# Expert rows gathered in quarters and turned by VectorE in blocks of 32x32

## What is computed

```python
for e in range(N_EXPERTS):
    he = jax.nn.silu(xt @ w_gate[e]) * (xt @ w_up[e])
    y = y + combine[:, e:e + 1] * (he @ w_down[e])
```

## Time and profile before

| what | value |
|---|---|
| median of the runs | 1838.65 us (three runs, 1836.47 to 1839.16) |
| span of the profiled execution | 1837.4 us |
| expert stage, first to last step | about 1526 to 1807 us |
| TensorE busy over the span | 1760.4 us (96%) |
| VectorE busy | 858.7 us (47%) |
| GpSimd busy | 235.1 us (13%) |

### The profile page before, as it was taken

The page is one execution under the profiler, slowest core; times in us unless marked ns, Lnnn a source line. Parts: engine busy times, 40 slices in busy tenths (PEclk is TensorE's granted clock), DMA queues, the critical chain, the costliest instruction groups (busy, mean ns, idle before and its releaser), DMA issues. The chain is left out here.

```text
span 1837.4 us, 22565 instructions
## 1 busy us (share of the span) xinstructions
PE 1760.4 (96%) x9024; PEld 1289.9 (70%) x9024; DVE 858.7 (47%) x1672; ACT 627.8 (34%) x1248; POOL 235.1 (13%) x286
## 2 busy tenths in 40 slices
PE   7999999999999999999999999999999989999993
PEld 6778888888888787568888888888766663333330
DVE  4436544543367345745554453263347562333224
ACT  5236344323353224635433332253347320000001
POOL 4000000000001003310000000000014404333322
PEclk9999999999999998999999999999999999999997
DMA  7223333332232217303333322332320158999974
GB/s 236 90 76 84 100 91 91 97 109 92 92 121 92 69 65 228 111 25 91 92 95 109 93 92 92 104 127 91 93 92 24 55 228 330 376 398 389 380 311 151
DMA packets 179528, 261.02 MB, mean 142 GB/s; under 512 B 18904, under 2 KB 134824, under 8 KB 167152
## 3 DMA queue, kind: packets, MB, share of 16 engines
q1 hardware_dynamic: 155824, 204.66, 33.2%
q0 software_dynamic: 19584, 25.77, 4.4%
q10 hardware_dynamic: 4032, 29.36, 4.1%
HBM read 297.53 MB, written 29.40 MB: 178 GB/s over the span
## 5 line engine op out<-in xcount | busy, mean ns | idle before, releaser
L189 PE MATMUL PB<-RING_R,OPS_R 128*128 128x512 f32 (+1 forms) x1056 | 414.7, 393 | 5.1 <-DVE RING_R L152 4.1
L191 PE MATMUL PB<-RING_R,OPS_R 128*128 128x512 f32 (+1 forms) x1056 | 409.1, 387 | 0.0
L190 PE MATMUL PB<-RING_R,OPS_R 128*128 128x512 f32 (+1 forms) x1056 | 408.9, 387 | 0.0
L169 DVE SCALAR_TENSOR_TENSOR RING_R<-RING,gains,RING_R 128x256 fp32r<-128x256 f32 (+2 forms) x456 | 219.4, 551 | 253.8 <-ACT RING_R L167 253.8
L189 PE MATMUL PB<-OPS_R,RING_R 128*128 128x512 f32 (+1 forms) x736 | 280.7, 381 | 0.0
L190 PE MATMUL PB<-OPS_R,RING_R 128*128 128x512 f32 (+1 forms) x736 | 279.5, 380 | 0.0
L191 PE MATMUL PB<-OPS_R,RING_R 128*128 128x512 f32 (+1 forms) x736 | 279.5, 380 | 0.0
L189 PEld LDWEIGHTS PB<-RING_R,OPS_R 128*128 128x128 f32 x1056 | 198.8, 188 | 48.4 <-DVE RING_R L152 5.3
L167 ACT ACTIVATE RING_R<-RING,gains 128x256 fp32r<-128x256 f32 (+2 forms) x456 | 209.9, 541 | 59.2 <-DMA RING<-in_w_in 47.7
L191 PEld LDWEIGHTS PB<-RING_R,OPS_R 128*128 128x128 f32 x1056 | 198.8, 188 | 40.7
L190 PEld LDWEIGHTS PB<-RING_R,OPS_R 128*128 128x128 f32 x1056 | 199.0, 188 | 38.9 <-issue 0.2
(11 more groups left out here) (379 smaller groups left out, 2033.1 us busy)
## 6 DMA issues: line engine op xcount, KB each, us to landing
RING<-in_ffn_w_gate SPq DMA_DIRECT2D x44, 512.0 KB, 4.0
RING<-in_ffn_w_up SPq DMA_DIRECT2D x44, 512.0 KB, 5.2
RING<-in_ffn_w_down SPq DMA_DIRECT2D x44, 512.0 KB, 4.2
RING<-in_w_expert_gate SPq DMA_DIRECT2D x16, 1024.0 KB, 8.0
RING<-in_w_expert_up SPq DMA_DIRECT2D x16, 1024.0 KB, 11.6
OPS<-in_w_expert_gate SPq DMA_DIRECT2D x16, 1024.0 KB, 13.6
OPS<-in_w_expert_up SPq DMA_DIRECT2D x16, 1024.0 KB, 16.2
Y<-in_w_expert_down ACTq DMA_DIRECT2D x14, 1024.0 KB, 9.6
```

The lines of the kernel that those rows point to most:

```text
L169: t = nc.vector.scalar_tensor_tensor(by_k(RING_R, o)[:, :, k, :], raw, g, high.bitcast(fp32), ALU.mult, ALU.subtract)
L189: nc.tensor.matmul(o, x[0], w[0], start=start, stop=False)
L190: nc.tensor.matmul(o, x[0], w[1], start=False, stop=False)
L191: return nc.tensor.matmul(o, x[1], w[0], start=False, stop=stop)
```

## The change

The rows are stored in their natural order (no stepped read any more). From step 2 on a pair's rows are not gathered as 128 rows of 4 KB but as four times 128 quarters of 1 KB: in DMA b, partition 32q + i receives quarter q of the row for slot 32b + i. A block of 32x32 words then holds 32 slots by 32 channels, and VectorE's block transpose puts the channels on the partitions (`quarters_T`, two instructions for a step, each of 128 x 512 words, reading with a step of eight words). TensorE's `turn_rows` and VectorE's `rows_T` remain for steps 0 and 1 only, where the source is now read with a step of eight words.

The indices of the quarters (`idx_quarters`, four columns for each pair) need slot indices moved between partitions. TensorE does this with 16 small products on a copy of the table as floats, in the middle of the last filler, and VectorE turns them into 4 x index + q. A gather of quarters waits for VectorE to have turned the buffer's former rows, where it waited for TensorE's transposes; VectorE's transposes wait for `gate_up(s)`, whose `XgT` they overwrite, and for the gather.

```diff
--- before.py
+++ after.py
@@ -212,6 +212,8 @@
                 return self.sem, v + self.base
 
 
+        QR = D // 4
+
         class Norm:
             def __init__(self, name, src, ready, parts, gain=None, rows=None, normed=True, split=True, deferred=False, direct=False):
                 self.direct = direct
@@ -270,9 +272,8 @@
 
             def rows_scaled(self, dve, m):
                 dve.wait_ge(*self.rec.at(m + 1))
-                turned = lambda x: x.rearrange("q (p k) -> q p k", k=KT)
-                nc.vector.scalar_tensor_tensor(Y[:, m, :].rearrange("q (k p) -> q p k", k=KT), turned(self.src[:, m, :]),
-                                               stat[:, 32 + m:33 + m], turned(self.rows), ALU.mult, ALU.mult
+                nc.vector.scalar_tensor_tensor(Y[:, m, :], self.src[:, m, :],
+                                               stat[:, 32 + m:33 + m], self.rows, ALU.mult, ALU.mult
                                                ).then_inc(self.xn.sem, 1)
 
             def reciprocals(self, dve, m):
@@ -2272,7 +2273,7 @@
         strict = Zr(P)
         o_io = o_[0]
         io128, iopair, tokid, pri = Zr(P), Zr(NPAIR), Zr(MT), Zr(EG)
-        io64, pair128, io7, iob, pidx = Zr(NE), Zr(NPAIR), Zr(7), Zr(NO), Zr(1)
+        io64, pair128, io7, iob, pidx, qidx = Zr(NE), Zr(NPAIR), Zr(7), Zr(NO), Zr(1), Zr(1)
         n_io = o_[0] - o_io
         lg = Zr(MT * 36).rearrange("p (m n) -> p m n", m=MT)
         L = lambda n: Zr(MT * n).rearrange("p (m n) -> p m n", m=MT)
@@ -2290,6 +2291,8 @@
         si = sb("slot_i", [P, 2, MT], i32)
         idxi = sb("idx_i", [P, NPAIR], i32)
         idxv = Zr(NPAIR)
+        idxf = Zr(NPAIR)
+        idx4 = sb("idx_quarters", [P, 4, NPAIR], i32)
         outi = sb("slot_rows", [P, NPAIR], i32)
         cnt7 = Zr(7 * NE).rearrange("p (e j) -> p e j", j=7)
         bex = Zr(NO * NE).rearrange("p (b e) -> p b e", e=NE)
@@ -2310,6 +2313,9 @@
         q_oh = sem("router_onehot")
         q_id = sem("router_index_mm")
         q_done = sem("router_done")
+        q_fl = sem("rows_as_numbers")
+        q_qm = sem("quarter_rows_mm")
+        q_qi = sem("quarter_rows_ready")
         q_out = sem("slot_rows_ready")
         s_h2 = sem("h2_rows_stored")
 
@@ -2364,14 +2370,20 @@
                     pe.wait_ge(q_oh, n // MT + 2)
                 t = nc.tensor.matmul(PB[:, 7, 0:NPAIR], ohp[:, n, :], ohb[:, n, :], start=(n == 0), stop=(n == 2 * MT - 1))
             t.then_inc(q_id, 1)
-            keep_busy(20)
+            keep_busy(10)
+            pe.wait_ge(q_fl, 1)
+            for b in range(4):
+                for q in range(4):
+                    t = nc.tensor.matmul(PB[q * 32:(q + 1) * 32, 5, b * NPAIR:(b + 1) * NPAIR], ident[:, b * 32:(b + 1) * 32], idxf,
+                                         start=True, stop=True)
+            t.then_inc(q_qm, 1)
+            keep_busy(10)
 
         last_rows = RAW.rearrange("p a b -> p (a b)")
 
         def router_last_rows(pool):
             pool.wait_ge(*q_ta.at(4))
-            nc.gpsimd.tensor_tensor(Y[:, MT - 1, :].rearrange("q (k p) -> q p k", k=KT), last_rows.rearrange("q (p k) -> q p k", k=KT),
-                                    n6.rows.rearrange("q (p k) -> q p k", k=KT), ALU.mult).then_inc(n6.xn.sem, 1)
+            nc.gpsimd.tensor_tensor(Y[:, MT - 1, :], last_rows, n6.rows, ALU.mult).then_inc(n6.xn.sem, 1)
 
         ROWS_BANK = (4, 5, 7)
 
@@ -2497,11 +2509,15 @@
             ch.add(nc.vector.tensor_scalar(idxv, PB[:, 7, 0:NPAIR], 0.0, SKIP, ALU.is_equal, ALU.mult))
             ch.wait()
             nc.vector.scalar_tensor_tensor(idxi[:], PB[:, 7, 0:NPAIR], -1.0, idxv, ALU.add, ALU.add).then_inc(q_done, 1)
+            nc.vector.scalar_tensor_tensor(idxf, PB[:, 7, 0:NPAIR], -1.0, idxv, ALU.add, ALU.add).then_inc(q_fl, 1)
             tt(bex, bend.unsqueeze(1).to_broadcast([P, NO, NE]), iob.unsqueeze(2).to_broadcast([P, NO, NE]), ALU.is_le)
             red(bexs, bex, ALU.add)
             ch.wait()
             nc.vector.tensor_scalar(widx[:], bexs, float(P), pidx, ALU.mult, ALU.add).then_inc(q_out, 1)
             nc.vector.scalar_tensor_tensor(outi[:], idxv, pidx, pair128, ALU.add, ALU.add).then_inc(q_out, 1)
+            dve.wait_ge(q_qm, 1)
+            nc.vector.tensor_scalar(idx4[:], PB[:, 5, 0:4 * NPAIR].rearrange("p (b n) -> p b n", b=4), 4.0, qidx, ALU.mult, ALU.add
+                                    ).then_inc(q_qi, 1)
 
 
         GU_WORDS, D_WORDS = 2 * 2 * KT * DE, 2 * 2 * D
@@ -2585,9 +2601,17 @@
             pool.wait_ge(m_z, 2)
             pool.wait_ge(s_h2, 16 * MT)
             pool.wait_ge(q_done, 2)
+            quarters = h2_dram.rearrange("t (a n) -> (t a) n", a=4)
+
+            def gather_quarters(s):
+                pool.wait_ge(m_te, 2 * (s - 1))
+                for b in range(4):
+                    nc.gpsimd.indirect_dma_start(
+                        Xg[:, s % 2, b * QR:(b + 1) * QR], None, quarters,
+                        bass.IndirectOffsetOnAxis(ap=idx4[:, b, pair_of[s]:pair_of[s] + 1], axis=0),
+                        bounds_check=4 * T - 1, oob_is_err=False).then_inc(m_g[s % 2], 16)
+
             def gather(s):
-                if s >= 2:
-                    pool.wait_ge(m_t, 2 * (s - 1))
                 nc.gpsimd.indirect_dma_start(
                     Xg[:, s % 2, :], None, h2_dram[:, :],
                     bass.IndirectOffsetOnAxis(ap=idxi[:, pair_of[s]:pair_of[s] + 1], axis=0),
@@ -2623,11 +2647,12 @@
             pool.wait_ge(q_out, 2)
             pool.wait_ge(m_fill, 16 * NPAIR)
             overflow_gate_up(0)
-            gather(2)
-            gather(3)
+            pool.wait_ge(q_qi, 1)
+            gather_quarters(2)
+            gather_quarters(3)
             for s in range(NSTEP):
                 if s + 4 < NSTEP:
-                    gather(s + 4)
+                    gather_quarters(s + 4)
                 if s % 3 == 1 and s + 4 < NSTEP:
                     overflow_gate_up(s // 3 + 1)
                 if s % 3 == 0:
@@ -2638,11 +2663,11 @@
             def turn_rows(s):
                 if s:
                     pe.wait_ge(m_te, 2 * s)
-                pe.wait_ge(m_g[s % 2], 16 * (s // 2 + 1))
+                pe.wait_ge(m_g[s % 2], 16)
+                rows = Xg[:, s % 2, :].rearrange("q (p k) -> q k p", k=KT)
                 for hf in range(2):
                     for k in range(4):
-                        t = nc.tensor.transpose(PB[:, hf, k * P:(k + 1) * P],
-                                                Xg[:, s % 2, (4 * hf + k) * P:(4 * hf + k + 1) * P], ident[:])
+                        t = nc.tensor.transpose(PB[:, hf, k * P:(k + 1) * P], rows[:, 4 * hf + k], ident[:])
                     t.then_inc(m_t, 1)
 
             def gate_up(s):
@@ -2658,6 +2683,8 @@
 
             def turn_hidden(s):
                 pe.wait_ge(m_h, s + 1)
+                if s == 1:
+                    pe.wait_ge(q_qi, 1)
                 for j in range(2):
                     t = nc.tensor.transpose(PB[:, 4 + s % 2, j * P:(j + 1) * P], Hh[:, s % 2, j * P:(j + 1) * P], ident[:])
                 t.then_inc(m_ht, 1)
@@ -2683,8 +2710,6 @@
             turn_rows(1)
             gate_up(0)
             for s in range(NSTEP):
-                if s + 2 < NSTEP:
-                    turn_rows(s + 2)
                 turn_hidden(s)
                 if s + 1 < NSTEP:
                     gate_up(s + 1)
@@ -2713,6 +2738,14 @@
                     nc.vector.tensor_copy(XgT[:, s % 2, 4 * hf:4 * hf + 4, :].rearrange("p k n -> p (k n)"), PB[:, hf, :]
                                           ).then_inc(m_te, 1)
 
+            def quarters_T(s):
+                dve.wait_ge(m_gu, s - 1)
+                dve.wait_ge(m_g[s % 2], 16 + 64 * (s // 2))
+                rows = Xg[:, s % 2, :].rearrange("q (b c k) -> q b k c", b=4, k=KT)
+                cols = XgT[:, s % 2].rearrange("p k (b r) -> p b k r", b=4)
+                for hf in range(2):
+                    nc.vector.transpose(cols[:, :, 4 * hf:4 * hf + 4], rows[:, :, 4 * hf:4 * hf + 4]).then_inc(m_te, 1)
+
             def hidden_T(s):
                 dve.wait_ge(m_ht, s + 1)
                 nc.vector.tensor_copy(HhT[:, s % 2].rearrange("p j n -> p (j n)"), PB[:, 4 + s % 2, 0:DE]).then_inc(m_he, 1)
@@ -2735,7 +2768,7 @@
             hidden(0)
             for s in range(NSTEP):
                 if s + 2 < NSTEP:
-                    rows_T(s + 2)
+                    quarters_T(s + 2)
                 hidden_T(s)
                 if s + 1 < NSTEP:
                     hidden(s + 1)
@@ -3035,7 +3068,7 @@
     each = lambda x: np.broadcast_to(np.asarray(x, f)[None], (P, len(x)))
     k["c_iotas"] = np.concatenate([
         each(np.arange(P) - P), each(np.arange(NPAIR) + 1), tq + 1, each(EG - np.arange(EG)), each(np.arange(NE) * HB),
-        each(np.arange(NPAIR) * P), each((np.arange(7) + 1) * HB), each(np.arange(NO)), p], axis=1).astype(f)
```

(1 more changed line is left out.)

## The result

The changed kernel takes 1848.8 us (median of 4 runs, 1848.16 to 1850.39) against 1838.91 for the kernel before (now four runs; the 1838.65 above is of three): a ratio of 1.0056, 95% interval 1.0045 to 1.0068. It is 10 us **slower**, a small change but clear of 1; the forecast was 5 us faster.

What follows compares the result with a forecast made beforehand. TensorE was taken to set the pace, with the DMA engines nearly full and taking over once the transposes leave. The earlier end of the loads gave 1837.4 - 5.1 = 1832.3 us of span, 1833.5 as median; range 1828.5 to 1835.

Steps and rivals of the forecast that it cites:

- TensorE's -18.7 us: Expert stage: the row transposes leaving TensorE's path take 21 x 0.89 = 18.7 us off it.
- VectorE's transposes: Expert stage: two per step at 1.1 us each, twice that as ceiling, hidden by TensorE's work.
- 15.6 to 27.3 us: it fits into 32.4 us: GpSimd's indirect DMAs per three steps go from 12 to 21, 1.30 us apart, and fit three steps without transposes.
- The DMA engines' +0.8 us per three steps: Expert stage: quarter records, skipped rows and more DMAs add 0.8 us, so three steps need 35.0 us of DMA time.
- The end of the loads: Last load lands at 1774.6; TensorE starts on pair 15's weights at 1775.4 instead of 1780.56: -5.1 us.
- The router's +2.0: Before the first rows: sixteen small products (2.0 us, 0.55 covered) and strided turns (0.5) add 2.0 us, from +0.6 to +5.
- gathers come late: Expert stage: GpSimd's 3024 records per three steps delay gathers, stalling VectorE and TensorE; 1845.5 us, up to 1858; chance 0.30.

Runs made afterwards that it cites:

- e6: e2 with only the first half of each down weight row loaded from step 2 on (results differ): 1826.36 us (0.9932).
- r1: The changed kernel once more, unaltered, on the same chip as r2 and r3: 1853.82 us (1.0068).
- e3: The changed kernel without the overflow gate and up loads after the first four: 1835.34 us (0.9972).
- e5: The kernel before with 3 to 10 spare indirect DMAs, all rows skipped, behind the overflow loads of every third step: 1853.93 us.
- r3: e5 once more, unaltered, on the same chip as r1 and r2: 1855.37 us.
- e2: The changed kernel with one whole-row indirect DMA per gather from step 2 on, VectorE's transposes kept (values differ): 1840.94 us (1.0005).
- e4: The changed kernel with the store of the rows ahead of the overflow gate and up loads in every third step: 1846.29 us (1.0033).
- e9: The changed kernel with GpSimd waiting for the next gate and up products before the quarters in steps 2, 5, ... 17: 1846.09 us (1.0047).
- e8: The changed kernel with the four overflow gate and up loads split two and two over two steps: 1858.44 us (1.0097).
- r2: e9 once more, unaltered, on the same chip as r1 and r3: 1846.05 us.
- c1: Against the kernel before: quarters and VectorE's transposes only in every third step, others gathered whole and turned by TensorE, products behind the first turns: 1834.5 us (0.998).
- e7: The changed kernel with the sixteen products and VectorE's index operation moved behind the first two steps' turns: 1846.93 us (1.0039).
- e10: The kernel before with the spare indirect DMAs of e5, each waited for before the next is issued: 1971.25 us.
- e11: The kernel before with 6 to 20 clears of a spare tile on GpSimd in place of the spare DMAs of e5: 1860.15 us.
- e12: e5 with three clears on GpSimd behind each spare DMA, so that they are issued about 2.5 us apart: 1904.68 us.

## Why the prediction was wrong

- **TensorE's -18.7 us** was right: 18.3 left its path, and e6 shows the 10.82 us step.
- **VectorE's transposes** at 1.1 us: measured 1086 ns. Hidden, as said. That it met the copy's 681 ns times the price of a stride may be luck: no run transposes without the stride.
- **"15.6 to 27.3 us: it fits into 32.4 us"** is the step that failed. GpSimd's issues were costed as its own time, and they do fit. What they do to others while they come without a pause was not in the sum: up to 5.6 us until TensorE's signal is seen, six times 3.1 us net. No row of before showed it, as its rows of DMAs hold no more than 8, and its signals came after 0.05 us. What the runs show in place of "it fits": behind rows of 16 the signal is late every time (six in the result, four in r1), with rows of at most 8 none in a step is (e3), and spare DMAs that move nothing bring late ones to the kernel before (e5, r3). Why a row of DMAs holds back TensorE's signal stays open.
- **The DMA engines' +0.8 us per three steps** was wrong as well. It rested on 444 records of 1 KB and 3024 in all; there are 1802, and the share stayed at 8.7%. That the weights are the next bound was right (e2, e6): without held signals the steps took 257.4 and 258.8 us in e3 and e2, 33.6 to 33.8 per three steps, not 35.0. Of TensorE's 18.3 us only 6.1 to 7.6 could thus be had.
- **The end of the loads**, the term that gave -5.1: gate and up on the last pair's weights (step 22) was to start at 1775.4. It starts at 1789.74, as each held signal also keeps SP from issuing the next loads; without held signals in the steps at 1781.05 (e2) and 1778.09 (e3). So even there this term was too good by 3 us or more; the first step comes 5.2 (e3) and 6.6 us (e2) later than before, where 2.0 were taken.
- **The router's +2.0** became +5.7: the products cost 0.45 (2.0 said), but two held signals and a clock at half behind them came on top.
- **The rival "gathers come late"** had the side right and 1845.5, near the 1848.8, by another mechanism. In the profiled run of the changed kernel nothing waited for a gather, so the near number is luck. Its mechanism does show where GpSimd falls behind or TensorE gets ahead: gathers come late in e3, e4 and e9 (21.6 to 22.9 us of waiting), and overflow loads or stores in e2, e4, e8, e9 and r1. Its count of 3024 records failed as the sum's did. The Trainium skill says in "DMA: Bandwidth & Descriptors", section "Queues, rings and completion order", that a DMA engine drains a whole packet, typically 9 to 17 descriptors, from one ring before it goes to the next. No run here shows that number; a record here holds four quarters.

## What to carry to other kernels

An engine with room to spare isn't a free place for indirect DMAs. Count how many GpSimd issues without a pause, and look at whether TensorE's signals still come 0.05 us after the work. Look in more than one execution: the same program (e9, r2) had none and nine held. When work leaves the bounding engine, ask for the next bound first (here the weights, 6 us away): moving a third of the turns won 4 us (c1), while moving all of them with one DMA a gather, and no signal held in a step, won none (e2).

## What was not expected of the hardware

- Signals of TensorE came up to 5.8 us after gate and up's records ended (e7), and TensorE halted after them, while GpSimd issued indirect DMAs 1.30 us apart. It was so 14 of 14 times in e5 and r3, in rows of 9 to 15 whose added DMAs moved nothing; never in e10, e11 and e12. In the same rows ScalarE's signals to VectorE came within 0.04 us of its work.
- It stays **open** why, and when: e9 had three rows of 18 without one, c1 six of 9, and the start of the changed kernel had two in a row of six. All traces without a held signal of programs with long rows are from two chips (3 and 8).
- Indirect DMAs whose rows are all skipped can still land late: TensorE waited for one of e8 until 14.7 us after its issue (1611.44 to 1626.11).
- Four 1 KB rows of one gather go as one record of 4 KB, and four skipped ones as one of 16 B (record sizes of the result's trace).
